# Two decoder blocks on one core: the last third of the first mixer issued in another order

## What is computed

```python
proj = rms_norm(x, mix_norm[l]) @ w_in[l]
rq, rk, rv, rg, c_q, c_kv, k_rope = split(proj)
# retention, 4 heads of 128, chunks of 128 rows
q, k = apply_rope(rq), apply_rope(rk) * dk ** -0.5
y = (q @ k.T * decay) @ v                       # within and across chunks
y_ret = rms_norm(y, ret_head_norm) * silu(rg)   # norm by head, then the gate
# latent attention, 8 heads
q = rms_norm(c_q) @ w_uq ; k, v = split(rms_norm(c_kv) @ w_ukv)
k_rope = apply_rope(rms_norm(k_rope, kn_rope))  # one rotated key for all heads
y_mla = softmax(causal(q @ k.T * scale)) @ v
x = x + concat(y_ret, y_mla) @ w_o[l]
```

## Time and profile before

| | |
|---|---|
| time, median of 3 runs | 1783.94 us (1783.86 to 1784.62) |
| the profiled execution | 1780.57 us, span from first to last instruction 1778.8 us |
| busy in the span | PE 86%, DVE 53%, ACT 36%, POOL 3% |
| the first mixer | about 203 to 336 us, its last third about 257 to 319 us |
| the second one | about 718 to 851 us, its last third about 772 to 834 us |

### The profile page before, as it was taken

The page is one execution under the profiler, slowest core; times in us unless marked ns, Lnnn a source line. Parts: engine busy times, 40 slices in busy tenths (PEclk is TensorE's granted clock), DMA queues, the critical chain, the costliest instruction groups (busy, mean ns, idle before and its releaser), DMA issues.

```text
span 1778.8 us, 30446 instructions
## 1 busy us (share of the span) xinstructions
PE 1538.4 (86%) x12249; PEld 1257.9 (71%) x12250; DVE 945.3 (53%) x1717; ACT 633.7 (36%) x1026; POOL 58.5 (3%) x71
## 2 busy tenths in 40 slices
PE   7999997999999999997999997996859666666666
PEld 7999886799989999885899986885744333333233
DVE  5666686466566666775665667764643222222222
ACT  5444564444444444563544457434310000000000
POOL 1000020000000000010200000000000000000000
PEclk9999998999999999998999998998979988888888
DMA  9555362265565554550555543442099999999996
GB/s 310 188 188 186 127 223 83 72 213 172 188 200 159 193 184 165 169 184 26 184 189 183 189 165 101 134 151 77 15 418 393 430 430 431 431 430 432 434 428 297
DMA packets 147225, 407.85 MB, mean 229 GB/s; under 512 B 5216, under 2 KB 98768, under 8 KB 138976
## 3 DMA queue, kind: packets, MB, share of 16 engines
q1 hardware_dynamic: 145888, 404.31, 61.3%
q0 software_dynamic: 1280, 2.75, 0.7%
HBM read 406.00 MB, written 1.05 MB: 229 GB/s over the span
## 4 chain that ended last, share of the span: by engine, by line
PE 60%; DMA 19%; DVE 9%; issue 5%; ACT 5%; POOL 1%; SPq 0%; POOLq 0%; DVEq 0%; ACTq 0%
DMA expert_gu<-in_exp_gu 19%; PE bank L1869 17%; PE bank L1870 17%; PE bank L1871 17%; PE bank L2448 4%; DVE wlo L1128 2%; ACT whi L702 2%; POOL small L627 1%; ACT prob L811 1%; PE bank L2464 1%; PE bank L2203 1%; DVE x L1185 1%; PE bank L2411 1%; ACT xn L716 1%; ACT hhi L710 0%
## 5 line engine op out<-in xcount | busy, mean ns | idle before, releaser
L1128 DVE TENSOR_TENSOR wlo<-raw,whi 128x1024 fp32r<-128x1024 f32 (+1 forms) x396 | 449.5, 1183 | 150.6 <-ACT whi L702 149.8
L1869 PE MATMUL bank<-hhi,whi 128*128 128x256 f32 x1504 | 427.7, 284 | 8.7 <-DVE hlo L1166 4.3
L1870 PE MATMUL bank<-hlo,whi 128*128 128x256 f32 x1504 | 426.6, 284 | 0.0
L1871 PE MATMUL bank<-hhi,wlo 128*128 128x256 f32 x1504 | 426.6, 284 | 0.0
L702 ACT ACTIVATE whi<-raw 128x1024 fp32r<-128x1024 f32 (+1 forms) x396 | 382.3, 1019 | 92.6 <-PE bank L1871 92.5
L1869 PEld LDWEIGHTS bank<-hhi,whi 128*128 128x128 f32 x1504 | 289.4, 192 | 13.0 <-issue 5.2
L1870 PEld LDWEIGHTS bank<-hlo,whi 128*128 128x128 f32 x1504 | 289.6, 193 | 3.1
L1871 PEld LDWEIGHTS bank<-hhi,wlo 128*128 128x128 f32 x1504 | 289.5, 192 | 0.0
L2448 PE MATMUL bank<-expert_gu,h_e 128*32 128x256 f32 x2112 | 169.9, 492 | 130.6 <-DMA expert_gu<-in_exp_gu 126.4
L2448 PEld LDWEIGHTS bank<-expert_gu,h_e 128*32 128x32 f32 x2112 | 84.6, 140 | 215.8 <-issue 194.4
L1817 DVE SCALAR_TENSOR_TENSOR e_sg<-e_th,bank 128x128 f32<-128x128 f32 x33 | 9.5, 287 | 305.2 <-ACT e_th L1084 305.2
(11 more groups left out here) (358 smaller groups left out, 1652.2 us busy)
## 6 DMA issues: line engine op xcount, KB each, us to landing
expert_gu<-in_exp_gu SPq DMA_DIRECT2D x32, 4096.0 KB, 37.9
expert_dn<-in_exp_dn SPq DMA_DIRECT2D x32, 2048.0 KB, 38.7
raw<-in_ffn_w_gate SPq DMA_DIRECT2D x44, 1024.0 KB, 5.5
raw<-in_ffn_w_up SPq DMA_DIRECT2D x44, 1024.0 KB, 7.4
raw<-in_ffn_w_down SPq DMA_DIRECT2D x44, 1024.0 KB, 4.9
raw<-in_w_in SPq DMA_DIRECT2D x36, 1024.0 KB, 5.1
raw<-in_w_o SPq DMA_DIRECT2D x8, 1024.0 KB, 5.3
raw<-in_w_out SPq DMA_DIRECT2D x4, 1024.0 KB, 5.2
```

Of the source, the lines that this page charges most:

```text
L1128: nc.vector.tensor_tensor(slot_view(wlo, slot, src), src, slot_view(whi, slot, src).bitcast(F32), ALU.subtract).then_inc(lo_ready, inc)
L1869: nc.tensor.matmul(o, sh, mh, start=first, stop=False, skip_group_check=shared)
L1870: nc.tensor.matmul(o, sh, ml, start=False, stop=False, skip_group_check=shared)
L1871: return nc.tensor.matmul(o, sl, mh, start=False, stop=last, skip_group_check=shared)
```

## The change

Five things are done, in both instances of the mixer.

1. The last third goes in pairs of rounds: scores 0 and 1, then 2 and 3, stand together on PE, maxima and exponentials likewise on DVE and ACT. Weight splits are moved behind them.
2. The low parts `low(0)` and `low(1)` stand right behind the gate on DVE, ahead of the maxima of round 2; on PE both weighted sums of a pair stand together, and scores 2 and 3 stand ahead of the first output product.
3. Retention's norm is separate from its gate: ACT multiplies the gain by the row's scale into a new tile `g_retr`; DVE writes output times root times `g_retr` to `yr` first, then (tanh + 1) times the gate's input to `gg`, and multiplies `yr` by `gg` later, between shares 2 and 3. The second gate multiplication is gone. The second output product waits for the norm, and only the last transposes for `yr`.
4. The key row is multiplied by its gain and rotated on GpSimd, between the six-column root and the 16-column powers. The row's own root is applied later, where DVE spreads the key over the heads (a copy before, a multiplication now). ACT waits for GpSimd's first multiplication before it writes squares over its input.
5. DVE rotates the first tile of query rows one split earlier, and PE does the key and value product by row tile, the first tile ahead of the wait for the rotated rows.

Two pairs of semaphores in the expert part are merged, which moves nothing. The diff without declarations:

```diff
@@ -673,9 +674,24 @@
...
                     rsqrt(6)
+                    n = 10 * kind_index(i) + 4
+                    hr = ROPE // 2
+                    lo_, hi_ = slice(0, hr), slice(hr, ROPE)
+                    nc.gpsimd.tensor_tensor(krn[:], b4[:, :, LAT:CB], g_k[:].rearrange("p (o d) -> p o d", o=1).broadcast_to([P, T, ROPE]),
+                                            ALU.mult).then_inc(qtab_ready, 1)
+                    gp.wait_ge(qtab_ready, n + 1)
+                    for c in (lo_, hi_):
+                        nc.gpsimd.tensor_tensor(krt[:, :, c], krn[:, :, c], sin_m[:], ALU.mult).then_inc(qtab_ready, 1)
+                    gp.wait_ge(qtab_ready, n + 3)
+                    for c in (lo_, hi_):
+                        ins = nc.gpsimd.tensor_tensor(krn[:, :, c], krn[:, :, c], cos_m[:], ALU.mult)
+                    ins.then_inc(qtab_ready, 1)
+                    gp.wait_ge(qtab_ready, n + 4)
+                    nc.gpsimd.tensor_tensor(krn[:, :, lo_], krn[:, :, lo_], krt[:, :, hi_], ALU.subtract).then_inc(qtab_ready, 1)
+                    nc.gpsimd.tensor_tensor(krn[:, :, hi_], krn[:, :, hi_], krt[:, :, lo_], ALU.add).then_inc(qtab_ready, 1)
                     rsqrt(16, r[:, 16:32], 16)
                     rsqrt(16, r[:, 32:48], 32)
-                    nc.gpsimd.tensor_tensor(r[:, 0:16], small[:, 1, 0:16], minus_half[:, 0:16], ALU.pow).then_inc(root_ready, 1)
+                    nc.gpsimd.tensor_tensor(small[:, 4, 32:48], small[:, 1, 0:16], minus_half[:, 0:16], ALU.pow).then_inc(root_ready, 1)
                     rsqrt(T * RH, r[:, 48:48 + T * RH], 48)
...
@@ -842,6 +858,7 @@
...
                 act.wait_ge(q_ready, 4 * z + 4)
+                act.wait_ge(qtab_ready, 10 * z + 5)
                 for t in range(T):
...
@@ -869,28 +886,30 @@
...
                 turned_heads(1, 1)
+                for t in range(T):
+                    nc.scalar.activation(g_retr[:, t, :], g_ret[:], ACT.Identity, scale=nr[:, 2, t:t + 1]).then_inc(gretr_ready, 1)
                 splits(26)
                 weights(0)
+                weights(1)
                 splits(27)
-                weights(1)
                 for t in range(T):
...
                     nc.scalar.activation(sqr[:, t, :], bank[1 + 2 * t][:], ACT.Square).then_inc(yrsq_ready, 1)
+                turned_weights(0)
                 splits(28)
-                turned_weights(0)
+                turned_weights(1)
                 product(13)
...
                     nc.scalar.activation(gg[:, t, :], bank[2 * t][:], ACT.Tanh, scale=nr[:, 2, t:t + 1]).then_inc(gth_ready, 1)
+                high(0)
+                high(1)
                 splits(29)
-                high(0)
-                turned_weights(1)
                 weights(2)
-                high(1)
+                weights(3)
                 splits(30)
-                weights(3)
-                splits(31)
                 turned_weights(2)
                 high(2)
+                splits(31)
                 turned_weights(3)
...
@@ -1321,8 +1340,6 @@
...
                                                        ALU.mult, ALU.mult).then_inc(latn_ready, 1)
-                link(*[nc.vector.scalar_tensor_tensor(krn[:, t, :], b4[:, t, LAT:CB], r[:, 4 + t:5 + t],
-                                                      g_k[:], ALU.mult, ALU.mult) for t in range(T)])
                 splits(7)
...
@@ -1330,18 +1347,12 @@
...
                                             ALU.subtract).then_inc(latlo_ready, 1)
-                splits(9)
+                splits(8)
                 dve.wait_ge(split_used, OPEN + mid_pos(i, 3, 1) + 1)
...
                 splits(13)
-                link(*[nc.vector.tensor_tensor(krt[:, :, k * hr:(k + 1) * hr], krn[:, :, k * hr:(k + 1) * hr], sin_m[:], ALU.mult)
-                       for k in range(2)])
-                link(*[nc.vector.tensor_tensor(krn[:, :, k * hr:(k + 1) * hr], krn[:, :, k * hr:(k + 1) * hr], cos_m[:], ALU.mult)
-                       for k in range(2)])
-                link(nc.vector.tensor_tensor(krn[:, :, 0:hr], krn[:, :, 0:hr], krt[:, :, hr:ROPE], ALU.subtract),
-                     nc.vector.tensor_tensor(krn[:, :, hr:ROPE], krn[:, :, hr:ROPE], krt[:, :, 0:hr], ALU.add))
 
...
@@ -1356,7 +1367,7 @@
...
                 splits(14)
-                dve.wait_ge(qtab_ready, 4 * z + 4)
+                dve.wait_ge(qtab_ready, 10 * z + 10)
                 qv = q[:].rearrange("p t (h d) -> p t h d", d=QD)[:, :, :, NOPE:QD]
...
@@ -1380,10 +1391,11 @@
...
                                                 per_head(32 + MH * t + 4 * h, 4).broadcast_to([P, 4, NOPE]), ALU.mult)
-                    nc.vector.tensor_copy(kt[:, :, NOPE:QD], krn[:, t:t + 1, :].broadcast_to([P, MH, ROPE])).then_inc(kf_ready, 1)
+                    nc.vector.tensor_scalar(kt[:, :, NOPE:QD], krn[:, t:t + 1, :].broadcast_to([P, MH, ROPE]), r[:, 4 + t:5 + t], None,
+                                            ALU.mult).then_inc(kf_ready, 1)
                 dve.wait_ge(root_ready, by_key + 1)
                 nc.vector.tensor_scalar(small[:, 4, 0:16].rearrange("p (h t) -> p t h", t=T),
-                                        r[:, 0:16].rearrange("p (t h) -> p t h", t=T), MLA_SCALE, None, ALU.mult)
+                                        small[:, 4, 32:48].rearrange("p (t h) -> p t h", t=T), MLA_SCALE, None, ALU.mult)
                 splits(18)
...
@@ -1392,43 +1404,44 @@
...
                 mask_scores(1)
-                splits(26)
                 largest(0)
...
                 mask_scores(3)
+                largest(1)
+                splits(26)
+                shares(0)
                 splits(27)
-                largest(1)
-                shares(0)
+                shares(1)
                 for t in range(T):
...
                 splits(28)
-                shares(1)
-                dve.wait_ge(gth_ready, 2 * z + 2)
-                link(*[nc.vector.scalar_tensor_tensor(gg[:, t, :], gg[:, t, :], 1.0, bank[2 * t][:], ALU.add, ALU.mult)
-                       for t in range(T)])
-                for t in range(T):
-                    nc.vector.scalar_tensor_tensor(gg[:, t, :], gg[:, t, :], nr[:, 2, t:t + 1], g_ret[:],
-                                                   ALU.mult, ALU.mult).then_inc(gg_ready, 1)
-                low(0)
-                splits(29)
+                dve.wait_ge(gretr_ready, 2 * z + 2)
                 dve.wait_ge(root_ready, roots[0])
-                dve.wait_ge(gg_ready, 2 * z + 2)
                 for t in range(T):
...
                         ins = nc.vector.scalar_tensor_tensor(yr[:, t, c], bank[1 + 2 * t][:, c], r[:, 48 + RH * t + h:49 + RH * t + h],
-                                                             gg[:, t, c], ALU.mult, ALU.mult)
-                    ins.then_inc(yret_ready, 1)
+                                                             g_retr[:, t, c], ALU.mult, ALU.mult)
+                    ins.then_inc(yrn_ready, 1)
+                dve.wait_ge(gth_ready, 2 * z + 2)
+                for t in range(T):
+                    nc.vector.scalar_tensor_tensor(gg[:, t, :], gg[:, t, :], 1.0, bank[2 * t][:], ALU.add, ALU.mult).then_inc(gg_ready, 1)
+                low(0)
+                low(1)
                 largest(2)
-                low(1)
+                largest(3)
+                splits(29)
+                shares(2)
+                dve.wait_ge(gg_ready, 2 * z + 2)
+                dve.wait_ge(yrn_ready, 2 * z + 2)
+                for t in range(T):
+                    nc.vector.tensor_tensor(yr[:, t, :], yr[:, t, :], gg[:, t, :], ALU.mult).then_inc(yret_ready, 1)
+                shares(3)
                 splits(30)
-                largest(3)
-                shares(2)
+                low(2)
                 splits(31)
-                shares(3)
-                low(2)
                 low(3)
...
@@ -2047,16 +2060,18 @@
...
 
-                pe.wait_ge(rowsq_ready, 2 * z + 2)
-                for job in (6, 7):
-                    for half in range(2):
-                        wh, wl = split_parts(job, half, S // 2)
-                        wh, wl = (w.rearrange("p k n -> p (k n)") for w in (wh, wl))
-                        for t in range(T):
-                            c = slice(t * P, (t + 1) * P)
+                for t in range(T):
+                    c = slice(t * P, (t + 1) * P)
+                    if t:
+                        pe.wait_ge(rowsq_ready, 2 * z + 2)
+                    for job in (6, 7):
+                        for half in range(2):
+                            wh, wl = split_parts(job, half, S // 2)
+                            wh, wl = (w.rearrange("p k n -> p (k n)") for w in (wh, wl))
                             ins = three(bank[4 + 2 * t + job - 6][:, half * S:(half + 1) * S], lat_hi[:, 2, c], lat_lo[:, 2, c],
                                         wh, wl, True, True)
-                        use(ins, job, half)
+                            if t:
```

(16 more changed lines are left out.)

25 lines of the change are left out of this document (13 added, 12 removed).

## The result

| | before | changed |
|---|---|---|
| time, median | 1783.9 us (1780.96 to 1784.62, 4 runs) | 1752.86 us (1750.81 to 1754.45, 4 runs) |
| the profiled execution, span | 1780.57, 1778.8 us | 1752.26, 1750.4 us |
| start of the router's product (PE) | 1306.99 us | 1276.03 us |

The change is faster, by 31.0 us: ratio 0.9828, interval 0.9811 to 0.9845. I had forecast 22.8 us, and the range ended at 1755. By the start of the router's product, which is the first thing behind both mixers that is placed the same in the two kernels, the gain in the profiled executions is 30.96 us.

A forecast was written before the change was run, and what follows sets the result against it. TensorE was taken as the bound, held up in the last third by chains run in series on in-order queues. Gains of 10.9 + 0.5 = 11.4 us a mixer, 22.8 for two, gave 1783.94 - 22.8 = 1761.1 us, range 1755 to 1770.

The forecast's parts named there:

- Step (b): Last third, norm apart from gate: root of 2.54 us ends at 286.8, low parts ready at 290.5 and 290.8.
- step (e): Clock in the last third: falls after 2.5 us idle, costing 1.7 us; 0.5 to 1.0 off leaves 10.9 a mixer.
- step (d): End of the last third: waits of 0.9 and 1.9 us for ACT's copies, next product near 306.7 instead of 318.95.
- The rival that was to turn the sign: First part: GpSimd's rotation operations delay the powers once each takes 2.5 us; at 4.5 us each, 1790 us; chance 2%.
- the walk: Last third reckoned part by part from priced operations: round 2 at 290.6, next product near 306.7.
- a second fall behind the waits of (d): End of last third: clock may fall again for another 1.7 us, of which before paid 0.6 us there.
- the walk over the old order: Last third of the kernel before at the same prices: 318.4 against 318.95, so 0.55 us taken off the gain.
- more comes through: Rival: clock falls at most once and 1.2 of the rotation's 1.74 us arrive; 13.5 to 14 a mixer, 1756; 10%.
- clock stays low longer: Rival, last third: low clock as long as before, then twice as long at the end; 7.3 us a mixer, 1769; 13%.

The follow-up runs named there:

- p1: Changed kernel with round 1's share multiplications moved on DVE behind the retention sums, to run beside GpSimd's root; 1751.87 us, one run.
- p2: Changed kernel with an unused 1024-column addition of two SBUF inputs on DVE, under way when GpSimd's eight-column root begins; 1754.16 us, one run.
- d1: Changed kernel with an unused 512-column addition on DVE in front of the low parts of rounds 0 and 1; 1758.86 us, one run.
- s3: Changed kernel with the old gate in two multiplications put back ahead of the low parts; 1757.87 us, ratio 0.9849.
- s1: Kernel before with only the mixer's first part changed (key rotation on GpSimd, earlier query rotation, key/value product by row tile); 1781.87 us, ratio 0.9988.
- d2: Changed kernel with an unused 1024-column addition on DVE in front of the low parts of rounds 0 and 1; 1756.41 us, one run.
- v1: Changed kernel with the low parts of rounds 0 and 1 ahead of the gate's multiplication on DVE; 1750.05 us, ratio 0.9824.

## Why the prediction fell short of the result, and where it was right

In short: the order of the waits was right, and the size was wrong by one price and what hangs on it. Step (b) took the root at 2.54 us where it cost 1.64, and step (e) therefore charged each mixer a fall of the clock that did not come.

**Right.** The 4.94 us in front of the first output product are gone, nothing new stands there, and the two waits for ACT's copies appear where step (d) put them (0.63 and 1.39 us, forecast 0.9 and 1.9). In the first part 0.5 us passes on and not 1.74, since DVE's queue sets the next stop: 251.45 went to 250.94. GpSimd's rotation shows no cost, and takes 2.7 us, not the 8.5 I allowed it; its rows:

```profile
223.52 0.32 POOL L680 TENSOR_TENSOR krn<-b,g_k 128x64 f32<-128x64 f32 x1
223.91 0.58 POOL L684 TENSOR_TENSOR krt<-krn,sin_m 128x32 f32<-128x32 f32 x2
224.57 0.58 POOL L687 TENSOR_TENSOR krn<-krn,cos_m 128x32 f32<-128x32 f32 x2
225.23 0.45 POOL L690 TENSOR_TENSOR krn<-krn,krt 128x32 f32<-128x32 f32 x1
225.64 0.57 POOL L691 TENSOR_TENSOR krn<-krn,krt 128x32 f32<-128x32 f32 x1
...
240.78 5.82 POOL L628 TENSOR_TENSOR small<-small,minus_half 128x16 f32<-128x16 f32 x2 [14.56 <-DVE small L1362]
```

GpSimd still idles 14.56 us before the powers. The row I took the price from the earlier trace rows was 2.42 us for two multiplications of 128x32; the rotation's pairs take 0.58. The trace of before had the second price too, for the same form, in the row just ahead of that one:

```profile
211.88 0.46 POOL L673 TENSOR_TENSOR q_tab<-cos_m,g_q 128x32 f32<-128x32 f32 x2
```

The rival that was to turn the sign needed 2.5 us and more for each operation and had no ground.

**Too small.** By job 15 the first mixer's last third really ended 14.65 - 0.5 = 14.15 us sooner, 3.25 more than the 10.9 I took. Setting the first part's 0.5 us aside, as the walk did, round 2 starts at 290.25 (290.6 in the walk) and job 15 at 304.80 (306.7).

Step (b), the root: 2.54 us taken, 1.64 measured. I had both prices in front of me, and had written down what would decide between them, then kept the larger one. p1 and p2 show the cause. The step also had the path wrong: the tanh by ACT comes last and not the root, so the dear root would have cost 0.58 us by itself (2.09 - 1.51), not 0.9.

Step (e), the clock, the larger one. I set the idle at 2.5 us and let the clock fall "as it did". The idle was 1.51 us, and there it mostly does not fall. From round 2 to job 15 the walk has 16.1 us: that is what p2 and d1 take with a fall (16.2), and the changed kernel takes 14.55. So the walk of this stretch was right in sum, in part by errors that cancel (its two waits came 0.78 us shorter, the work between them as much longer), and 1.55 us of it was a fall that did not happen. With the root at its dear price, in p2, each mixer is 0.58 + 1.65 = 2.2 us longer, and this is the larger part of the 3.25.

The rest is in two deductions. I had taken 0.5 to 1.0 us off for a second fall behind the waits of (d); none came. And I had taken off 0.55 us by which the walk over the old order was short, but the walk over the new order was not short: 16.1 against 16.2 where the clock falls. In all 0.35 (round 2 sooner) + 1.55 + 0.8 + 0.55 = 3.25. That the idle came out a full 1.0 us shorter than I had it is in part chance: 0.35 is round 2 sooner, and 0.65 is PE ending its weighted sums later than in the walk (288.74 against 288.1).

The kernel before has a second fall at the end of the last third. Up to job 15 it is contained in the 318.95 that the sum starts from; behind that it was not counted. Its stretches, PE alone, show it:

```profile
314.00:316.00 2.00, 1.42 (x8) 0.50 0.00 0
316.00:318.00 2.00, 2.00 (x11) 0.50 0.00 0
318.00:320.00 2.00, 2.00 (x10) 0.50 0.00 0
320.00:322.00 2.00, 2.00 (x10) 0.98 0.00 0
```

The clock is at its lower level until about 320, beyond the first product of job 15 at 318.95. The first three matmuls of that product take 1.30 us there (318.95 to 320.25) and 0.80 in the changed kernel (304.30 to 305.10). Hence the gain grows behind it, from 14.65 us to 15.2 at the first wide product of the second mixer (724.15 before, 708.94 after). Summed for the first mixer: 0.5 (first part) + 14.15 (last third, to job 15) + 0.55 (behind it) = 15.2, against 11.4; by the router it is 30.96 for both.

The rival "more comes through", 1756, is the one that came nearest. Its half on the rotation did not come true, its half on the clock did, and the time went beyond it. I had given it 10% and argued against it with DVE's queue in the first part; the clock was the half that mattered, and I had no argument against that. The rival "clock stays low longer" has its place too: s3 is such a kernel, with 17.88 us in its second mixer alone, and even it reaches 1757.87 us.

**What was not in the sum.** The forecast added the gain to the median, as if both kernels' medians lay equally far above their profiled executions. They lie 3.3 and 0.6 us above, and this makes 2.7 of the 8.2 us between forecast and result; by the profiled execution the forecast was 1757.8 and the time 1752.26, 5.5 us apart. What the other runs of before spend their time on no trace shows. In the trace of s1, whose last third is the old one, the stretch from round 2 to job 15 takes 1.7 us more over both mixers than in that of before, with the same idle ahead.

Not all of the gain at the router reaches the end. The first experts' product, before and then changed:

```profile
1333.39 3.66 PE L2448 MATMUL bank<-expert_gu,h_e 128*32 128x256 f32 x64 [1.20 <-DVE h_e L1807]
```

```profile
1302.62 5.34 PE L2464 MATMUL bank<-expert_gu,h_e 128*32 128x256 f32 x64 [1.19 <-DVE h_e L1820]
```

The same 64 matmuls take 1.7 us longer, and the clock in the stretch is 0.50 after (1304 to 1306) and 1.00 before (1335 to 1337). So 1.7 of the 30.96 us are given back there in the profiled executions, and the products behind it keep the delay. It is 5.06 to 5.59 us in all eleven other kernels with the new last third and 3.66 us in s1, whose last third is the old one, so it is no accident of one execution. Another 0.9 us go at the very end, with the last experts' product, before and then changed:

```profile
1760.16 5.35 PE L2448 MATMUL bank<-expert_gu,h_e 128*32 128x256 f32 x64 [4.65 <-DMA expert_gu<-in_exp_gu]
```

```profile
1730.93 6.22 PE L2464 MATMUL bank<-expert_gu,h_e 128*32 128x256 f32 x64 [5.46 <-DMA expert_gu<-in_exp_gu]
```

This product too goes by the clock: 0.50 in 1732 to 1736 of the changed kernel, 1.00 in 1738 to 1742 of d2. It takes 3.66 us in d2, p1, p2 and v1 and 6.09 to 6.33 us in the other kernels with the new last third. The stretch from the router's product to the last instruction follows it: 471.8 to 471.9 us in those four, 474.2 and more in the others. That is why d2, with the longer idle, ended sooner than d1, and why a single run here ranks nothing closer than 3 us. What decides the clock at these two places was not tried and stays open.
